# A decoder layer with a product-key expert stage: work moved across three stage boundaries, and a new order of scaling, evacuating and gathering inside the expert stages

## What is computed

```
q = (xt @ w_pq).reshape(T, H, 2, PEER_HALF)
s = jnp.einsum('thpd,hpkd->thpk', q, sub_keys)
s1, i1 = lax.top_k(s[:, :, 0], K); s2, i2 = lax.top_k(s[:, :, 1], K)
top_s, pos = lax.top_k(s1[..., :, None] + s2[..., None, :], K)   # 16 of 256, per head
g = softmax(top_s)
a = gelu(einsum('cd,ced->ce', xb, u_tab[idx])) * g
y = einsum('ce,ced->cd', a, v_tab[idx])
```

## Time and profile before

| | us |
|---|---|
| median of 3 runs | 3259.08 |
| lowest and highest | 3255.02, 3262.56 |
| profiled execution | 3264.28 |
| its span | 3262.5 |
| PE busy | 3002.5 (92%) |
| DVE busy | 2468.9 (76%) |
| POOL, ACT busy | 1435.6, 1196.3 |
| mean granted clock of PE | 0.971 |

### The profile page before, as it was taken

The page is one execution under the profiler, slowest core; times in us unless marked ns, Lnnn a source line. Parts: engine busy times, 40 slices in busy tenths (PEclk is TensorE's granted clock), DMA queues, the critical chain, the costliest instruction groups (busy, mean ns, idle before and its releaser), DMA issues. The chain is left out here.

```text
span 3262.5 us, 42577 instructions
## 1 busy us (share of the span) xinstructions
PE 3002.5 (92%) x15866; PEld 2696.6 (83%) x15866; DVE 2468.9 (76%) x4383; ACT 1196.3 (37%) x2213; POOL 1435.6 (44%) x878
## 2 busy tenths in 40 slices
PE   8996998996888899999999998949999999999997
PEld 6886887886888899999999998937788887887886
DVE  4125774447999988888888876649898898979888
ACT  2112332111222456656556555523333333333331
POOL 4113220004666443344343444455665656566662
PEclk9998998998999999999999999969999999999998
DMA  4214222225777665665666667778787888878882
GB/s 168 94 68 147 92 81 83 78 68 178 241 242 245 208 213 214 226 219 209 226 219 214 225 217 270 281 269 307 271 306 268 303 274 291 289 262 298 277 290 97
DMA packets 294056, 695.57 MB, mean 213 GB/s; under 512 B 20464, under 2 KB 136560, under 8 KB 290672
## 3 DMA queue, kind: packets, MB, share of 16 engines
q1 hardware_dynamic: 190960, 316.66, 29.7%
q0 software_dynamic: 73728, 268.47, 23.4%
q10 hardware_dynamic: 29184, 108.01, 8.4%
HBM read 565.13 MB, written 127.93 MB: 212 GB/s over the span
## 5 line engine op out<-in xcount | busy, mean ns | idle before, releaser
L1077 PE MATMUL z_ps<-hT_hi,u_hi 128*128 128x384 f32 x2048 | 708.2, 346 | 60.7 <-POOL u_lo L794 34.8
L1078 PE MATMUL z_ps<-hT_lo,u_hi 128*128 128x384 f32 x2048 | 692.1, 338 | 0.0
L1079 PE MATMUL z_ps<-hT_hi,u_lo 128*128 128x384 f32 x2048 | 692.0, 338 | 0.0
L1381 PE MATMUL y_ps<-v_hi,a_hi 128*128 128x512 f32 x1536 | 603.1, 393 | 64.8 <-DVE a_lo L1482 44.1
L794 POOL TENSOR_TENSOR u_lo<-u_raw,u_hi 128x1024 fp32r<-128x1024 f32 x128 | 313.9, 2453 | 685.0 <-ACT u_hi L790 684.3
L1382 PE MATMUL y_ps<-v_lo,a_hi 128*128 128x512 f32 x1536 | 600.6, 391 | 0.0
L1383 PE MATMUL y_ps<-v_hi,a_lo 128*128 128x512 f32 x1536 | 600.2, 391 | 0.0
L1432 POOL TENSOR_TENSOR v_lo<-room,v_hi 128x1024 fp32r<-128x1024 f32 x128 | 341.2, 2666 | 245.8 <-ACT v_hi L1409 244.2
L1077 PEld LDWEIGHTS z_ps<-hT_hi,u_hi 128*128 128x128 f32 x2048 | 391.4, 191 | 65.5 <-POOL u_lo L794 39.5
L1381 PEld LDWEIGHTS y_ps<-v_hi,a_hi 128*128 128x128 f32 x1536 | 289.9, 189 | 134.1 <-DVE a_lo L1482 44.2
L1078 PEld LDWEIGHTS z_ps<-hT_lo,u_hi 128*128 128x128 f32 x2048 | 390.9, 191 | 0.0
(11 more groups left out here) (187 smaller groups left out, 4964.9 us busy)
## 6 DMA issues: line engine op xcount, KB each, us to landing
u_raw<-in_uT SPq DMA_DIRECT2D x128, 512.0 KB
room<-in_v SPq DMA_DIRECT2D x128, 512.0 KB
z<-z_sb ACTq DMA_DIRECT2D x128, 384.0 KB
gates<-g_sb ACTq DMA_DIRECT2D x24, 2048.0 KB
z_in<-z SPq DMA_DIRECT2D x16, 1536.0 KB
g_in<-gates SPq DMA_DIRECT2D x16, 1536.0 KB
room<-z SPq DMA_DIRECT2D x15, 1536.0 KB
room<-gates SPq DMA_DIRECT2D x15, 1536.0 KB
```

Source lines behind the costliest of these rows:

```text
L1077: nc.tensor.matmul(o, u_hi[e][:, k], hT_hi[:, k, cols], start=(k == 0), stop=False)
L1078: nc.tensor.matmul(o, u_hi[e][:, k], hT_lo[:, k, cols], start=False, stop=False)
L1079: last = nc.tensor.matmul(o, u_lo[e][:, k], hT_hi[:, k, cols], start=False, stop=(k == KT - 1))
L1381: nc.tensor.matmul(o, ah, v_hi[p][:, i, c], start=(i == 0), stop=False)
```

## The change

```diff
...
@@ -904 @@
+                    else:
+                        act.wait_ge(tiles.u_here[0], 16)
+                        tiles.hi(0)
@@ -914 @@
-                turns(act, PH, turn)
-                act.wait_ge(tiles.u_here[0], 16)
-                tiles.hi(0)
-                act.wait_ge(gaps, 1)
-                tk.exp().then_inc(exps, 1)
+                turns(act, PH, turn, last=2)
@@ -959 @@
-                    for p in range(2):
-                        tk.side(link, p, h, tk.s_cp[:, p])
-                    tk.pairs(link, h)
+                    if not last:
+                        for p in range(2):
+                            tk.side(link, p, h, tk.s_cp[:, p])
+                        tk.pairs(link, h)
+                        if h % 2:
+                            tk.names(link, h // 2)
@@ -969 @@
-                tk.gaps().then_inc(gaps, 1)
-                for two in range(PH // 2):
-                    tk.names(link, two)
-                v.wait_ge(exps, 1)
-                tk.gates(link)
...
@@ -985 @@
-    PER_TURN = [44, 44, 24, 24, 24, 24, 24, 48]
+    SLOTS = 32
+    PER_TURN = [28, 40, 27, 27, 27, 27, 27, 53]
+    GATE_SLOTS = [SLOTS - 2] * (DB - 1) + [21]
+    PRODUCTS_AT = [28, 28, 29, 29, 30, 31]
...
+            first = 4 if s == 0 else 0
+            before, n = sum(PER_TURN[:s]), SLOTS - first
+            return range(before + PER_TURN[s] * max(k - first, 0) // n, before + PER_TURN[s] * max(k + 1 - first, 0) // n)
+        def steps_at(s, k):
+            if s < GB or k < 1:
+                return range(0)
+            n, first = GATE_SLOTS[s - GB], SLOTS * (s - GB)
+            k = min(k - 1, n)
+            return range(first + SLOTS * k // n, first + SLOTS * min(k + 1, n) // n)
...
@@ -1091 @@
-                    for q in range(Q):
-                        m, gm = s * Q + q, (s - GB) * Q + q
-                        z_half(m, 0)
-                        if q == 0 and s >= GB:
+                    for k in range(SLOTS):
+                        z_half(s * Q + k // 8, k % 8)
+                        for step in steps_at(s, k - 1):
+                            gates(step)
+                        if k == 0 and s >= GB:
...
@@ -1102 @@
-                        for n in range(1, 8):
-                            z_half(m, n)
-                            if s >= GB:
-                                gates(gm, n - 1)
-                        if s >= GB:
...
-                                wait(act, z_stored[e], 16 * (2 * m + j))
-                            nc.scalar.activation(z_sb[e][:, a * HT:(a + 1) * HT], z_ps[e][a][:, 0:HT],
-                                                 ACT.Copy).then_inc(z_read[e], 1)
-                            if a == 1:
-                                act.wait_ge(z_read[e], 2 * (2 * m + j) + 2)
-                                act.dma_start(d["z"][4 * m + 2 * j + e], z_sb[e][:]).then_inc(z_stored[e], 16)
-                            if s < TB - 1 and q == Q - 1 and n == 6:
-                                act.wait_ge(gaps, s + 1)
-                                tk.exp().then_inc(exps, 1)
...
-                                if n:
-                                    take_gates(gm, n - 1)
-                                if n == 1 and gm:
-                                    store_gates(gm - 1)
-                        if s >= GB:
-                            take_gates(gm, 7)
-                store_gates(Q * DB - 1)
+                    for k in range(SLOTS):
+                        m, n = s * Q + k // 8, k % 8
+                        j, e, a = n // 4, n // 2 % 2, n % 2
+                        if a == 0 and 4 * m + n // 2 < NK - 1:
+                            split_u(m, n // 2 + 1)
+                        for step in steps_at(s, k):
+                            scale_hot(step)
+                        act.wait_ge(z_done[e], 2 * (2 * m + j) + a + 1)
+                        if a == 0:
+                            wait(act, z_stored[e], 16 * (2 * m + j))
+                        nc.scalar.activation(z_sb[e][:, a * HT:(a + 1) * HT], z_ps[e][a][:, 0:HT],
+                                             ACT.Copy).then_inc(z_read[e], 1)
+                        if a == 1:
+                            act.wait_ge(z_read[e], 2 * (2 * m + j) + 2)
+                            act.dma_start(d["z"][4 * m + 2 * j + e], z_sb[e][:]).then_inc(z_stored[e], 16)
+                        if s == 0 and k == 1:
+                            act.wait_ge(gaps, 1)
+                            tk.exp().then_inc(exps, 1)
+                        if s < TB - 1 and k == SLOTS - 2:
+                            act.wait_ge(gaps, s + 2)
+                            tk.exp().then_inc(exps, 1)
+                        for step in steps_at(s, k - 1):
...
@@ -1258 @@
+                def first_product(t):
+                    c = slice(t * P, (t + 1) * P)
+                    v.wait_ge(ahead.g_here, 32)
+                    v.wait_ge(ahead.gelu_in, t + 1)
+                    zs = ahead.z_in[:, :, c].rearrange("p i (c t) -> p i c t", t=GT)
+                    gs = ahead.g_in[:, 4 * t:4 * t + 4].rearrange("p c (i t) -> p i c t", t=GT)
+                    nc.vector.tensor_tensor(zs, zs, gs, ALU.mult).then_inc(ahead.prod_in, 1)
+                for p in range(2):
+                    tk.side(link, p, PH - 1, tk.s_cp[:, p])
+                tk.pairs(link, PH - 1)
+                tk.gaps().then_inc(gaps, 1)
+                tk.names(link, PH // 2 - 1)
+                v.wait_ge(exps, 1)
+                tk.gates(link)
...
-                        chain.restart()
+                    for k in range(SLOTS):
+                        if k == 1 and s >= GB:
+                            v.wait_ge(found_T, s - GB + 1)
+                            nc.vector.tensor_copy(iT[:], g_ps[0][:, 0:2])
+                            link(nc.vector.tensor_copy(gT[:], g_ps[0][:, 2]))
+                        for step in steps_at(s, k):
+                            make_hot(step)
+                        if s < TB - 1:
+                            top_piece(s, k // 8, k % 8)
+                        for i in own_rows(s, k):
+                            dot(i)
+                        if s == TB - 1:
+                            for t in range(DB):
+                                if PRODUCTS_AT[t] == k:
+                                    first_product(t)
+                        if k % 8 == 7:
...
@@ -1322 @@
-            base, more = divmod(ROWS, NG - 1)
-            first = r * base + min(r, more)
-            return range(first, first + base + (r < more)) if r < NG - 1 else range(0)
+            return range(ROWS * max(r - 1, 0) // (NG - 2), ROWS * r // (NG - 2)) if r < NG - 1 else range(0)
...
+                for part in (range(GROUP // 2), range(GROUP // 2, GROUP)):
+                    for s in range(4):
+                        if part[0] == 0:
+                            pe.wait_ge(a_lo_in, s + 1)
+                        for a in range(2):
+                            turn(0, s, a, part)
...
+                split_v(0, 0)
+                hi(0, 0)
+                split_v(0, 1)
+                for s in range(1, DB - 1):
+                    hi(0, s)
+                split_v(0, 2)
+                split_v(0, 3)
+                hi(0, DB - 1)
...
-                        act.wait_ge(rest_here, 16)
+                    act.wait_ge(z_here[p], 32 * ((r + 1) // 2))
...
@@ -1430 @@
-                    for i in range(GROUP):
+                    for i in range(r == 0, GROUP):
@@ -1434 @@
+                            if k + EARLY < ROWS:
+                                gather(k + EARLY)
+                    if r == 0:
...
-                for r in range(NG):
+                v.wait_ge(v_hi_in[0], 1)
+                nc.vector.tensor_tensor(v_lo[0][:, 0], v_raw[0][:], v_hi[0][:, 0].bitcast(F32),
+                                        ALU.subtract).then_inc(v_lo_in[0], 1)
+                for s in range(DB):
+                    lo(0, s)
+                v.wait_ge(rows_gelu, 1)
+                link(nc.vector.tensor_tensor(a_rows[:], a_rows[:], ahead.picked_g[:], ALU.mult))
+                v.wait_ge(h_here, 16)
+                nc.vector.tensor_scalar(y[:], y[:], ALPHA, None, ALU.mult).then_inc(h_scaled, 1)
+                v.wait_ge(h_scaled, 1)
+                for r in range(1, NG):
...
@@ -1508 @@
+                        if r == NG - 1 and s % 2 and s // 2 < GB:
+                            v.wait_ge(added[s // 2], PH * TOPK)
+                            finish(s // 2)
...
```

212 lines of the change are left out of this document (89 added, 123 removed).

## The result

The changed kernel takes 3130.68 us (median of 4 runs, 3129.32 to 3134.64); the kernel before took 3260.82 beside it (4 runs). The ratio is 0.9594, interval 0.9556 to 0.9632: faster, by 130 us. The forecast was 3112, the range 3068 to 3163. The profiled execution took 3134.64 us, span 3132.8, against 3264.28 and 3262.5 before, so 129.7 us of span are to be found.

A forecast was written before the change was run, and what follows sets the result against it. DVE was taken to bound turns 0 and 1, PE with its waits the rest. Gains 20.3 + 28 + 32 + 5 + 34.4 + 0 + 20 + 7 = 147 us gave 3117, as a median 3112 us; range 3068 to 3163.

The forecast's parts named there:

- Step 1: Boundary from score to experts_in: moving the names off the way to the barrier gains 20.3 us; the last store is late next.
- first half of step 5: Boundary from experts_in to experts_out: PE's 44.1 us wait becomes 9.7 (store, barrier, three short operations), a gain of 34.4 us.
- Step 2: Turns 0 and 1 of experts_in: DVE limits; 20 fewer rows, less the moved search, gain 28 us, bounds 22 and 60.
- Step 3: Turns 2 to 6: placing steps a half apart removes most waits for one-hots; gain 32 us, bounds 10 and 42.
- Step 4: Turn 7 of experts_in: loses waits for one-hots but has more to do; gain 5 us, bounds 14 and minus 15.
- second half of step 5: Start of experts_out: h, asked for earlier behind z and gates, costs PE 0 us, bounds 0 and minus 4.
- Step 6: Output rounds: gathers two rows ahead remove most of DVE's waits for rows; gain 20 of 33 us, bounds 28 and 0.
- Step 7: The end: normalising blocks 0 and 1 inside the last round hides it; gain 7 us, bounds 9 and 0.
- the rounds gain nothing: Rival, chance 0.14: DMA engines limit rows in output rounds and the last round hides no norm; 3139 us.
- DVE late in the dense turns: Rival, chance 0.18: DVE stays late in experts_in, turns 0 to 6 gain only 22 and 10 us; 3140 us.
- More than I count: Rival, chance 0.16: turns 0 and 1 and the rounds come near PE's rate, gains 48, 38 and 27 us; 3079 us.

## Why the prediction was right, and where it wasn't

**Step 1** held, 19.7 us for 20.3: what was late next was the last store, as the trace of before had said.

**The first half of step 5** came out, 33.0 us for 34.4, in part by luck. The three short operations took 3.0 us, as counted, but the store wasn't what came last. It landed after 3.6 us, where 5 was taken, and the barrier waited some 4 us longer for DVE's last row, which the prediction doesn't name. With 38 rows in turn 7 ACT starts 2.9 us after the issue of the last store, and the whole gap is 6.4.

**Step 2** had the mechanism right (DVE's rows set the time) and a term too small. The dots fell by 30.9 us (152.4 to 121.5), close to the 34.6 forecast, and the search took 12.9. But DVE's idle time fell from 31.9 to 18.1 us, 13.8 in place of the 6 that I put under the search: its waits ahead of dots for which no releaser is named went from 11.4 to 1.3. Another 7 us came from DVE's own operations, which the prediction left out: the wide multiplication of a names piece (L752) took 26.8 us in eight, up to 4.1 each beside POOL's subtraction, and 11.1 in nine with the change, 1.23 each; the sums of the pairs grew from 6.7 to 13.7. That the new order misses the subtractions there was not planned. The 4 us by which the moved search could have been longer did not come: its multiplications took 1.2 and 1.3 us. A row is worth 1.0 us here, by the two runs with fewer, and not the 1.73 of its dot.

**Step 3** had the size nearly right and the late engine wrong in half of the waits. The 20 waits in five turns were one for each group of eight, as read, and went with the place of the steps, as forecast; but in ten of them DVE was late, behind its names piece, not ACT behind the evacuation. That was to be seen in the trace of before too, in the pair at 1299 us:

```profile
1296.53 1.29 DVE L1245 TENSOR_TENSOR hot<-near,iT 128x512 f32<-128x512 f32 x2
...
1297.85 1.28 ACT L1129 ACTIVATE hot_g<-hot,gT 128x128 f32<-128x128 f32 x4 [1.55 <-DVE hot L1245]
```

ACT stood idle 1.55 us there, released by DVE's one-hots, and 0.6 to 1.6 us in ten of the 20. In the other ten it stood idle only 0.41, of which the issue of its store takes 0.33, so there ACT was about as late as DVE. I had read the order of ACT's instructions for it and not these rows. The step left 2 us of wait in a turn, and none remained: of the 39.5 us gained 34.4 are these waits, and 5 are PE's own time (817.6 to 812.4 us busy).

**Step 4** failed. It counted 7 us of waits that go, and put the price of five more rows into the lower bound (15) only. PE's waits in turn 7 rose from 11.6 to 18.1 us instead. Rows were what it had no room for: the run with 38 shows 26 us.

**The second half of step 5** failed: h at 0, bounds 0 and minus 4. In the trace after, y is scaled at 2070.6, 32.6 us after ACT's first operation behind the barrier, where it was 29 us before: 3 MB of z and gates stand ahead of the 4 MB of h, and asking earlier doesn't make up for them. That the scaling and the waiting for h would lie behind the first matmul was part of the prediction; that DVE would have to make up for them to the end of the stage was not.

```profile
2070.59 4.43 DVE L1536 TENSOR_SCALAR y<-y 128x8192 f32<-128x8192 f32 x1 [19.22 <-DMA y<-h]
```

**Step 6** was right that early gathers win (26 us, forecast 20). It took DVE's 100.3 us of waiting (126.8 with the other buffers) as time to be had, and noted that DVE had no slack, but priced no contention: the operations grew by most of what the waits lost. From the first output matmul on only 8.5 us remain, and DVE's sums say why: the early gathers win 26, and h's wait and scaling, 19.2 + 4.4 us that had stood ahead of the first matmul, now stand in DVE's time. 26 less 23.6 is 2.4; the stretch of output matmuls fell by 3 (1079.0 to 1076). This is a sum that fits and not a test: neither of the two runs with an earlier h is faster, and DVE then waits for the gelu of round 1 and for PE instead. What would shorten DVE's start is open.

**Step 7** failed: the norms aren't hidden by moving them, since DVE is the bound in the last round too. The tail behind the last output matmul is shorter (15.9 us for 21.3), but the run with the norms at the end shows no loss that can be told from none.

**The rivals.** Of the two for which I gave 0.18 and 0.14, "the rounds gain nothing" is the one that came nearest, though not for its reason: the gathers gain 26 us, and DVE's start takes them back. "DVE late in the dense turns" was wrong for 27 rows; with 31 PE waits again for gates (8.3 us) and one-hots (5.1). "More than I count" came true in part, in turns 0 to 6. That the total was near is in part luck: 18 us of gain not counted stand against 35 counted too many.
